# Unit-matrix products on TensorE ahead of two stages of a hybrid transformer block

## What is computed

```python
mix = _mixers(n1, w_in, ...)                       # gated delta rule | convolution
h = h + mix @ w_out                                # out stage
h = h + _hierarchical_moe(_rmsnorm(h, g_moe), ...) # 64 experts, top 2
ple_gate = sigmoid(_rmsnorm(h, g_ple) @ w_ple_gate)
h = h + ple_gate * (p @ w_ple_proj)                # final stage
return _rmsnorm(h, g_final)
```

## Time and profile before

| | before |
|---|---|
| median of 3 runs | 1296.61 us (1296.58 to 1297.21) |
| the profiled execution, its own time | 1297.5 us |
| its span, first to last instruction | 1295.5 us |
| PE busy | 1118.0 us, 86% |
| DVE, ACT, POOL busy | 626.7, 322.1, 247.7 us |
| mean granted clock of PE | 0.946 |
| memory traffic | 272.54 MB read, 33.82 MB written |

### The profile page before, as it was taken

The page is one execution under the profiler, slowest core; times in us unless marked ns, Lnnn a source line. Parts: engine busy times, 40 slices in busy tenths (PEclk is TensorE's granted clock), DMA queues, the critical chain, the costliest instruction groups (busy, mean ns, idle before and its releaser), DMA issues.

```text
span 1295.5 us, 16743 instructions
## 1 busy us (share of the span) xinstructions
PE 1118.0 (86%) x6246; PEld 731.7 (56%) x6246; DVE 626.7 (48%) x931; ACT 322.1 (25%) x691; POOL 247.7 (19%) x347
## 2 busy tenths in 40 slices
PE   5999899999688885999899978888889987784996
PEld 4888688887577774888543323333323333233885
DVE  5699989985678865432451111101111111116764
ACT  5211211115545544322231100001001100004332
POOL 4000100002745651000112111111112111101220
PEclk9999999999799987999799989889999999896998
DMA  6111112100000102833799999999999999998531
GB/s 215 34 37 45 33 50 63 48 19 1 1 2 1 67 2 78 322 130 114 294 349 425 422 423 425 423 424 424 425 424 421 422 424 425 425 417 316 195 114 65
DMA packets 72472, 289.69 MB, mean 224 GB/s; under 512 B 12825, under 2 KB 38618, under 8 KB 55770
## 3 DMA queue, kind: packets, MB, share of 16 engines
q1 hardware_dynamic: 59344, 266.92, 51.8%
q0 software_dynamic: 9456, 16.80, 3.5%
q10 hardware_dynamic: 3610, 5.11, 1.1%
HBM read 272.54 MB, written 33.82 MB: 236 GB/s over the span
## 4 chain that ended last, share of the span: by engine, by line
DMA 26%; PE 19%; issue 3%; DVE 3%; SPq 0%; POOL 0%; ACT 0%; ACTq 0%; POOLq 0%; DVEq 0%
DMA qkvT<-in_w_up_dram 15%; DMA wup<-in_w_up_dram 9%; PE ps_u L2582 8%; PE ps_y L94 5%; PE ps_y L2603 2%; PE ps_pp L2030 1%; DMA y_rows<-xgT,si_x 1%; DMA convT<-y_rows 1%; PE ps_u L2626 1%; PE ps_xg L2571 1%; DMA y_rows<-qkvT,si 1%; PE ps_xg L2667 0%; SPq L1804 0%; PE ps_y L2638 0%; DVE hT L2207 0%
## 5 line engine op out<-in xcount | busy, mean ns | idle before, releaser
L2582 PE MATMUL ps_u<-wup,xgT 128*64 128x512 f32 x704 | 171.4, 643 | 37.5 <-DMA wup<-in_w_up_dram 34.6
L94 PE MATMUL ps_b<-n_hi,wh 128*128 128x512 f32 x384 | 157.5, 410 | 1.5 <-DVE wl L431 1.5
L2201 DVE TENSOR_TENSOR hb<-sil,ps_u 128x256 f32<-128x256 f32 x32 | 13.5, 421 | 288.2 <-ACT sil L2475 288.2
L94 PE MATMUL ps_b<-n_hi,wl 128*128 128x512 f32 x384 | 151.5, 394 | 0.0
L94 PE MATMUL ps_b<-n_lo,wh 128*128 128x512 f32 x384 | 151.4, 394 | 0.0
L2582 PEld LDWEIGHTS ps_u<-wup,xgT 128*64 128x64 f32 x704 | 56.3, 148 | 150.9 <-issue 141.2
L2582 PE MATMUL ps_u<-qkvT,xgT 128*64 128x512 f32 x320 | 75.7, 628 | 12.5 <-DMA qkvT<-in_w_up_dram 12.5
L94 PE MATMUL ps_y<-wg_hi,hx 128*128 128x512 f32 x256 | 83.5, 403 | 2.8 <-DVE hx L2278 2.8
L94 PEld LDWEIGHTS ps_b<-n_hi,wh 128*128 128x128 f32 x384 | 73.1, 190 | 17.0 <-issue 3.1
L94 PEld LDWEIGHTS ps_b<-n_hi,wl 128*128 128x128 f32 x384 | 72.7, 189 | 16.2
L94 PEld LDWEIGHTS ps_b<-n_lo,wh 128*128 128x128 f32 x384 | 73.2, 191 | 15.0 <-issue 1.0
(11 more groups left out here) (381 smaller groups left out, 2051.6 us busy)
## 6 DMA issues: line engine op xcount, KB each, us to landing
wup<-in_w_up_dram SPq DMA_DIRECT2D x44, 2048.0 KB, 33.8
qkvT<-in_w_up_dram SPq DMA_DIRECT2D x20, 2048.0 KB, 34.8
zT<-in_w_down_dram SPq DMA_DIRECT2D x22, 1024.0 KB, 34.9
convT<-in_w_down_dram SPq DMA_DIRECT2D x22, 1024.0 KB, 34.7
wraw<-in_w_in_dram SPq DMA_DIRECT2D x24, 512.0 KB, 4.2
qkvT<-in_w_down_dram SPq DMA_DIRECT2D x10, 1024.0 KB, 34.0
wdn_h<-in_w_down_dram SPq DMA_DIRECT2D x10, 1024.0 KB, 38.0
convT<-y_rows SPq DMA_DIRECT2D x16, 512.0 KB, 5.5
```

Source lines behind the costliest of these rows:

```text
L94: ins = nc.tensor.matmul(ps, lhs[a], rhs[b], start=first and k == 0, stop=last and k == 2)
L2201: nc.vector.tensor_tensor(hb[k][rows], sil[k][rows], ps_u[k][rows, FE:2 * FE], ALU.mult).then_inc(s_h, 1)
L2582: last = nc.tensor.matmul(ps_u[k][HC[c], :], xgT[k][:, j, HC[c]], wup[w][c][:, j, :], start=j == 0, stop=j == NJ - 1)
```

## The change

Two helpers multiply the 128x128 unit matrix `ident` (float32) with itself. The results are never read: the first helper writes into `ps_T`, which the transposes overwrite later, the second into the first 128 columns of `ps_g`, which the first product overwrites. In the out stage 18 such products stand at the head of `out_both`. In the final stage there are 59: five behind each of the 8 counts of `s_wg_hi`, five behind `s_wg_lo`, five behind the first `f_y1`, five behind the first transposes and four behind the first `f_hi`. `transposes(0)` moves behind the waits for `s_y0`, `s_y1`, `s_wg_lo` and `f_y1`.

```diff
@@ -1726,6 +1726,10 @@
             @blk.tensor
             def _(pe):
+                def keep_busy(n):
+                    for _ in range(n):
+                        nc.tensor.matmul(ps_T[:, 0, :], ident[:], ident[:], start=True, stop=True)
+
                 def out_half(t, g, h):
@@ -1735,6 +1739,7 @@
                 def out_both():
+                    keep_busy(18)
                     for j in range(NJ):
                         pe.wait_ge(s_wo_lo, j + 1)
@@ -2676,10 +2681,23 @@
-                transposes(0)
+                def keep_busy(bank, n):
+                    for _ in range(n):
+                        nc.tensor.matmul(bank, ident[:], ident[:], start=True, stop=True)
+
                 pe.wait_ge(s_y0, NPR)
                 pe.wait_ge(s_y1, NPR)
+                for j in range(NWJ):
+                    pe.wait_ge(s_wg_hi, j + 1)
+                    keep_busy(ps_g[:, 0, 0:P], 5)
                 pe.wait_ge(s_wg_lo, NWJ)
+                keep_busy(ps_g[:, 0, 0:P], 5)
+                pe.wait_ge(f_y1, 1)
+                keep_busy(ps_g[:, 0, 0:P], 5)
+                transposes(0)
+                keep_busy(ps_g[:, 0, 0:P], 5)
+                pe.wait_ge(f_hi, 1)
+                keep_busy(ps_g[:, 0, 0:P], 4)
                 for t in range(NT):
                     pe.wait_ge(f_lo, t + 1)
```

## The result

| | before | changed |
|---|---|---|
| median of ten runs each, us | 1297.33 (1295.52 to 1298.10) | 1300.00 (1297.85 to 1303.79) |
| ratio, 95% interval | | 1.0027 [1.0017, 1.0037] |
| profiled execution, us | 1297.5 | 1299.62 |
| its span, us | 1295.5 | 1297.7 |
| mean granted clock of PE | 0.946 | 0.953 |

A forecast was written before the change was run, and what follows sets the result against it. PE was taken to bound the out stage, with its first tile's loss passed on whole. Out stage +2.9 us plus final stage 0, laid on the median 1296.61, gave 1299.5 us, range 1297.7 to 1301.9.

The forecast's parts named there:

- Only some 1.2 us between the two counts: Out stage: most of PE's 8.92 us idle lies before `o_ml`; about 1.2 us between it and the first `wo_lo`.
- Price of a pass, 0.218 and 0.111 us: Out stage: one unit-product pass takes 0.218 us at half clock, 0.111 at full; 18 products are 36 passes.
- I take the value seen in this same place, 5.7 us: Out stage: clock rises after 5.7 us, first tile 2.9 us later; a rise after 3.4 us gives +1.8 us.
- The 13 half-clock products that they save are worth 2.7 us: Out stage: running those 13 products at full clock saves only 2.7 us, while the fillers take 6.8.
- fourth rival: Out stage: fillers cheap, last `wo_lo` bounds the first tile, 1.5 us sooner; total -2.0 us, 1294.6; chance 0.04.
- What PE's first tile loses, the whole stage loses: Out stage: PE is busy 95.50 of 95.80 us, so the first tile's delay passes on whole.
- moves as a whole: Expert stage: its transfers start only when the block is over, so it shifts with the out stage's end.
- The final stage: `low(1)` is late next, -0.5 to +1.2: Final stage: `low(1)`, behind a `y_rows` transfer, limits the gain to -0.5 us; a clock fall gives +1.2; 0 taken.
- Moved transposes and fillers "hidden": Final stage: moving the groups costs nothing, covered by 1.6 us, or 0.4 us with a half-clock start.
- Rival 1, the clock falls in the new wait: Final stage: clock falls in the new wait before `product(1, 0)`, +1.7 us; total 4.1 to 4.7, 1301.0; chance 0.17.
- Rival 2, the profiled before was unlucky: Out stage: with an earlier clock rise, before ends its first tile 1.1 us sooner; loss 4.0 us, 1300.6; chance 0.12.
- Rivals 3, 4 and 5: Out stage: 3, unit products don't raise the clock, +6.6 us, 0.06; 4, fillers cheap, 0.04; 5, delay absorbed, 0.10.

The follow-up runs named there:

- out_6: Against the kernel before: 6 unit products at the head of the out stage, behind the `o_ml` wait, final stage unchanged; ratio 1.0001, +0.1 us.
- out_54: Against the kernel before: 54 unit products at the head of the out stage, behind the `o_ml` wait, final stage unchanged; ratio 1.0085, +11.0 us.
- out_18: Against the kernel before: the change's 18 unit products in the out stage alone, final stage unchanged; ratio 1.0018, +2.3 us.
- six_fin: Whole change with 6 unit products in the out stage in place of 18; against the kernel before, ratio 0.9997, -0.4 us.
- out_12: Against the kernel before: 12 unit products at the head of the out stage, behind the `o_ml` wait, final stage unchanged; ratio 1.0021, +2.7 us.
- early_18: Against the kernel before: 18 unit products in front of the wait for `o_ml`, final stage unchanged; ratio 1.0001, +0.1 us.
- fin_59: Against the kernel before: the change's final stage alone, 59 unit products and moved transposes, out stage unchanged; ratio 0.9995, -0.6 us.
- fin_59_again: Same code as fin_59, measured once more beside fin_gap_again; against the kernel before, ratio 1.0000, 0.0 us.
- fin_gap_again: Same code as fin_gap, measured once more beside fin_59_again; against the kernel before, ratio 1.0004, +0.5 us.
- fin_order: Against the kernel before: final stage's moved waits and transposes without any unit product, out stage unchanged; ratio 1.0002, +0.3 us.
- fin_gap: fin_59 plus 9 unit products in front of `product(1, 0)`, behind a wait for `f_sg0`; against the kernel before, ratio 1.0012, +1.6 us.
- both_new: Against the kernel before: 16 unit products in front of the `o_ml` wait, the final stage's 59, and 9 before `product(1, 0)`; ratio 0.9998, -0.3 us.

## Why the prediction was right, point by point

Forecast 1299.5 us, slower; measured 1300.00, and by the two medians +2.7 us for the +2.9 of the sum. The absolute figure is close in part by luck: it was laid on a median of three runs, 1296.61, and the ten runs have 1297.33. The agreement of the sum is also better than that of its terms, as the points below show.

- **"Only some 1.2 us between the two counts."** Right: PE's idle time is 7.70 us, and the fillers start 0.06 us behind `mix_lo`.
- **Price of a pass, 0.218 and 0.111 us.** Right: 0.215 in out_6, and 108 passes in 14.44 us in out_54 (23 at half clock in 5.0 us, 85 in 9.5).
- **"I take the value seen in this same place, 5.7 us."** For the profiled changed kernel it was 3.5, by the low end of 3.4, and the first tile ended 1.5 us late, below the +1.8 of that case. With fillers behind `o_ml` the rise came 3.5 (changed, out_6), 4.8 (out_18), 5.0 (out_54), 5.8 (six_fin) and 5.9 us (out_12) after the first one; without fillers, in six profiles, between 4.7 and 5.9 us after the first real product. The one profile that I had did not show this scatter. The term for 18 is 2.3 us in the mean of Out; 2.9 was 0.6 too high.
- **"The 13 half-clock products that they save are worth 2.7 us."** Yes in the changed kernel: counted from `o_ml` its first real product comes 5.75 us later instead of 1.28, and Out is 16.50 instead of 14.71, so 4.47 - 1.79 = 2.7 us were saved. But early_18 shows that with them saved and nothing in the way the tile still ends hardly sooner, since the weights come no sooner. The prediction had that bound only in its fourth rival.
- **"What PE's first tile loses, the whole stage loses", and the expert stage "moves as a whole".** Shown by out_54 and, with the sign turned, by six_fin. In the single profile of the changed kernel it can't be seen: its router transposes met the full clock, and its last pair of experts began at 1154.39, in the execution of before at 1154.28; between SP's issue behind the out stage and the first `wg_hi` lay 535.6 us there and 536.1 before, in out_54 537.7. In all fourteen profiles it is 535.6 to 538.2 (six_fin), a scatter as large as the delay.
- **The final stage: `low(1)` is late next, -0.5 to +1.2.** Right on what bounds it: Fin is 10.13 with the fillers in three of four profiles of 59 products (-0.4 against the 10.56 of before), and the time did not move (-0.6 and 0.0 us, each with more than 1 us to either side). Too narrow at the top: the changed kernel's own profile has Fin 12.93. Of the 2.8 us above 10.13, 1.24 are a transfer of `y_rows` that landed late (DVE's second addition at 1199.64; in fin_59 it came 1.39 us behind the first, which would be 1198.40), and 1.56 the clock, which fell in the wait of 3.12 us (1209.94 - 1202.71 = 7.23 us for the 24 products, 5.67 in fin_59).
- **Moved transposes and fillers "hidden".** Yes in time: the fillers in front end at 1181.6, the transposes start at 1182.93. But "the clock holds" failed in the stretch before the transposes: in four of the seven profiles with 59 or more products they ran at half clock (1.97 us), behind waits of 1.35 to 2.47 us that the fillers leave open. In one of the four it cost 1.2 us.
- **Rival 1, the clock falls in the new wait (0.17).** It did in the changed kernel's profile. In fin_59, fin_59_again and six_fin, with waits of 1.71, 1.40 and 1.83 us, it did not. It can add to the loss in some executions, and may be why the changed kernel lost more than out_18 (+3.5 against +2.3, which the intervals do not separate). It is not the cause: out_18 has no such wait and nearly the whole loss, and fin_59 has the wait and no loss.
- **Rival 2, the profiled before was unlucky (0.12).** A little: its Out is 0.2 above the mean of six. Among those six the half-clock products at this place are 13, 13, 11, 11, 11 and 14. The Trainium skill, page "TensorE: Matmul & The Clock Gate", section "What's actually happening", has 6, 11 or 14 such products from run to run for a kernel of its own. That the count varies is so here too; 11 and 14 were seen at this place, 6 was not, and the lowest Out among the six is only 0.5 us below that of the profiled before.
- **Rivals 3, 4 and 5** fell: the unit products do raise the clock (0.98 from 513.70 on), they cost what the rows gave, and nothing absorbs.

## What to carry to other kernels

Filling PE's wait to raise its clock can pay only if the fillers end before the awaited work is ready and if the clock, not the next input, bounds what follows; no version here got that far. So read how much of an idle time lies behind the wait at which the fillers stand, and what the first real work waits for next. Here 1.2 us were open and 5.7 to 6.3 were filled, and even fillers placed in idle time gave back nothing that could be measured. A fixed number of fillers can become a delay in an execution in which its gap is shorter or the clock lower than in the profile it was sized by, as in fin_gap_again.

## What the runs showed of the hardware

- After PE went to work behind a wait, the clock rose to 2.4 GHz between 2.9 us (fin_order, from 1186.27) and 5.9 us (out_12, from 509.51) later. It differs from one execution to the next of the same code: 4.8 and 5.9 us in fin_gap and fin_gap_again, from the first product of the out stage.
- One DMA issue on ACT (L1637, `w_expert_router`) took 0.60 us in ten of the fourteen profiles and 1.91, 1.79, 1.65 and 1.50 us in out_18, early_18, out_54 and both_new. It stands in front of ACT's `mix_hi`, so `o_ml` and all behind it moved by as much. Out begins behind it and does not contain it. Both kernels with early fillers are among the four, which may be chance; I did not test it, and whether the measured times of these four kernels contain some of it is not known.
- Waits through which the clock held and in which it fell overlap in length: it held through the 2.42 us in front of the transposes of fin_59, and had fallen behind the 0.88 and 1.35 us at the same place of the changed kernel. Nearly equal waits went both ways: 2.42 us held and 2.41 fell (fin_59 and fin_59_again, the same code), and behind 0.91 and 1.35 us it held in both_new.
